# Up-projection blocks of a two-layer decoder: the last low part comes from an adding GpSimd DMA instead of a VectorE subtraction

## What is computed

```python
D_MODEL, SEQ, DEPTH = 2048, 256, 2
D_FF = 4 * D_MODEL

def sq_relu_mlp(h, w_up, w_down):
    return jnp.square(jax.nn.relu(h @ w_up)) @ w_down

for l in range(DEPTH):
    ...
    x = x + sq_relu_mlp(rms_norm(x, mlp_norm_g[l]), w_up[l], w_down[l])
```

## Time and profile before

| | us |
|---|---|
| median of 2 runs | 2017.7 (2017.51 and 2017.88) |
| span of the profiled execution | 2017.5 |
| PE busy | 2008.2 |
| PE weight load busy | 1680.1 |
| DVE busy | 1520.8 |
| ACT busy | 980.1 |
| POOL busy | 13.2 |

### The profile page before, as it was taken

How to read it: one execution, slowest core, us unless ns; L and a number is a source line. 1 busy time by engine, 2 the same in 40 slices (tenths; PEclk the granted TensorE clock), 3 DMA queues, 4 the chain that set the end, 5 groups by cost and what they waited for, 6 DMA issues and landing times.

```text
span 2017.5 us, 26213 instructions
## 1 busy us (share of the span) xinstructions
PE 2008.2 (100%) x9284; PEld 1680.1 (83%) x9284; DVE 1520.8 (75%) x2217; ACT 980.1 (49%) x1263; POOL 13.2 (1%) x21
## 2 busy tenths in 40 slices
PE   9999999999999999999999999999999999999998
PEld 7888888888888888888888998888888888888887
DVE  7789998887568558757888787888558757855875
ACT  6555555444344434434446665554444434444443
POOL 0000000000000000000000000000000000000000
PEclk9999999999999999999999999999999999999999
DMA  8655555655555655655565554565655555565563
GB/s 297 214 170 189 181 167 176 209 194 193 193 190 179 209 189 185 208 189 185 188 208 172 139 150 146 198 219 188 208 188 187 204 191 187 175 218 188 168 219 114
DMA packets 218034, 381.98 MB, mean 189 GB/s; under 512 B 15600, under 2 KB 40560, under 8 KB 217968
## 3 DMA queue, kind: packets, MB, share of 16 engines
q1 hardware_dynamic: 217104, 379.03, 56.9%
q10 hardware_dynamic: 864, 2.10, 0.3%
HBM read 379.00 MB, written 2.10 MB: 189 GB/s over the span
## 4 chain that ended last, share of the span: by engine, by line
PE 97%; issue 2%; DVE 0%; ACT 0%; POOL 0%; POOLq 0%; DVEq 0%; ACTq 0%
PE acc L473 29%; PE acc L475 29%; PE acc L474 29%; PE acc L493 2%; PE acc L494 2%; PE acc L495 2%; PE acc L749 1%; PE acc L750 1%; PE acc L751 1%; PE side L802 0%; PE side L792 0%; PE side L560 0%; DVE wlo L1365 0%; PE side L571 0%; PE side L775 0%
## 5 line engine op out<-in xcount | busy, mean ns | idle before, releaser
L1365 DVE TENSOR_TENSOR wlo<-raw,whi 128x1024 fp32r<-128x1024 f32 (+2 forms) x700 | 836.2, 1212 | 357.2 <-ACT whi L896 353.8
L896 ACT ACTIVATE whi<-raw 128x1024 fp32r<-128x1024 f32 (+2 forms) x700 | 726.3, 1050 | 708.2 <-PE acc L475 677.1
L473 PE MATMUL acc<-whi,opB 128*128 128x512 f32 x1296 | 505.5, 390 | 0.0
L475 PE MATMUL acc<-whi,opB 128*128 128x512 f32 x1296 | 504.4, 389 | 0.0
L474 PE MATMUL acc<-wlo,opB 128*128 128x512 f32 x1296 | 504.2, 389 | 0.0
L473 PE MATMUL acc<-whi,opA 128*128 128x512 f32 (+2 forms) x1296 | 501.8, 387 | 0.0
L475 PE MATMUL acc<-whi,opA 128*128 128x512 f32 (+2 forms) x1296 | 501.0, 387 | 0.0
L474 PE MATMUL acc<-wlo,opA 128*128 128x512 f32 (+2 forms) x1296 | 501.0, 387 | 0.0
L475 PEld LDWEIGHTS acc<-whi,opB 128*128 128x128 f32 x1296 | 243.2, 188 | 50.7
L473 PEld LDWEIGHTS acc<-whi,opB 128*128 128x128 f32 x1296 | 243.3, 188 | 50.4 <-DVE wlo L1365 0.3
L474 PEld LDWEIGHTS acc<-wlo,opB 128*128 128x128 f32 x1296 | 243.3, 188 | 50.1
(11 more groups left out here) (256 smaller groups left out, 1109.0 us busy)
## 6 DMA issues: line engine op xcount, KB each, us to landing
raw<-in_w_up SPq DMA_DIRECT2D x128, 1024.0 KB, 5.3
raw<-in_w_down SPq DMA_DIRECT2D x128, 1024.0 KB, 5.0
raw<-in_a_w_qkv SPq DMA_DIRECT2D x44, 1024.0 KB, 5.1
raw<-in_a_w_o SPq DMA_DIRECT2D x16, 1024.0 KB, 5.0
raw<-in_b_w_o SPq DMA_DIRECT2D x16, 1024.0 KB, 5.0
raw<-in_w_ukv SPq DMA_DIRECT2D x32, 256.0 KB, 4.3
raw<-in_w_dkv SPq DMA_DIRECT2D x4, 1024.0 KB, 5.1
raw<-in_b_w_dq SPq DMA_DIRECT2D x4, 768.0 KB, 4.7
```

Of the source, the lines that this page charges most:

```text
L473: mm(o, a_hi, w_hi, start=first and c == 0, stop=False)
L475: done = mm(o, a_lo, w_hi, start=False, stop=last and c == chunks - 1)
L896: done = fn(whi[:, place:place + ch, 0:n], raw[:, r, c0:c0 + ch, 0:n], ACT.Copy)
L1365: done = tt_(wlo[:, place:place + ch, 0:n], raw[:, r, c0:c0 + ch, 0:n], whi[:, place:place + ch, 0:n].bitcast(F32), ALU.subtract)
```

## The change

In the up blocks alone, half 7's low part is made in another way. ACT rounds `raw` into `whi` as before, and right after it writes `-raw`, rounded, into `wlo` (a second `ACTIVATE`, which increments the new `neg_ready`). DVE leaves out its split of half 7. POOL waits for `neg_ready` and issues a DMA that adds the raw tile (2 chunks, 128x1024 float32, 512 KB) onto `wlo` in SBUF, which leaves raw minus high. Its landing increments `lo_summed` by 16. PE waits for `lo_summed` ahead of half 7, and SP ahead of the next load into quad 3 of `raw`. DVE's split of half 6 increments `lo_ready` by 2. SP's loops are rolled otherwise, so that these waits can be written; its loads have the same order.

```diff
@@ sync
-            def whole(b, w, col, row=0):
+            def whole(b, w, col, row=0, summed=None):
                 for r in range(4):
+                    if r == 3 and summed is not None:
+                        sp.wait_ge(lo_summed, 16 * summed)
                     quad(b, r, w[:, bass.ds(row + 4 * r, 4), bass.ds(col, NB)])
@@ gpsimd
+            def up_lo(l):
+
+                for n in range(JB * QUARTERS):
+                    pool.wait_ge(neg_ready, JB * QUARTERS * l + n + 1)
+                    pool.dma_start(wlo[:, 6:8, :].bitcast(F32), raw[:, 3, 2:4, :],
+                                   accum_op=ALU.add).then_inc(lo_summed, 16)
@@ tensor, up blocks
+                def lo_ready_last(n, also=None):
+                    def ready(hf):
+                        if also:
+                            also(hf)
+                        if hf == 7:
+                            pe.wait_ge(lo_summed, 16 * n + 16)
+                    return ready
@@ scalar, split
                 done.then_inc(hi_ready, 1)
+                if kind == "up" and hf == 7:
+                    fn(wlo[:, place:place + 2, :], raw[:, r, c0:c0 + 2, :], ACT.Copy, scale=-1.0).then_inc(neg_ready, 1)
@@ vector, split
+                if kind == "up" and hf == 7:
+                    return
                 dve.wait_ge(hi_ready, 8 * b + hf + 1)
...
-                done.then_inc(lo_ready, 1)
+                done.then_inc(lo_ready, 2 if kind == "up" and hf == 6 else 1)
```

More of the change, by code:

```diff
@@ L252, in trunk @@
         lo_ready = sem("lo_ready")
+        neg_ready = sem("neg_ready")
+        lo_summed = sem("lo_summed")
         pe_halves = sem("pe_halves")
@@ L371, in mlp, with up, down @@
             def mlp(l):
-                with sp.Fori(0, QUARTERS) as q:
-                    with sp.Fori(0, JB) as j:
-                        whole(B_MLP[l] + 2 * JB * q + j, W_UP[l], D * q + NB * j)
+                def up(q, j):
+                    n = JB * QUARTERS * l + JB * q + j
+                    whole(B_MLP[l] + 2 * JB * q + j, W_UP[l], D * q + NB * j,
+                          summed=None if isinstance(n, int) and n == 0 else n)
+                def down(q):
+                    with sp.Fori(0, JB) as j:
+                        whole(B_MLP[l] + 2 * JB * q + JB + j, W_DOWN[l], NB * j, row=KC * q,
+                              summed=JB * QUARTERS * l + JB * q + JB)
+                for j in range(JB):
+                    up(0, j)
+                with sp.Fori(0, QUARTERS - 1) as q:
+                    down(q)
                     with sp.Fori(0, JB) as j:
-                        whole(B_MLP[l] + 2 * JB * q + JB + j, W_DOWN[l], NB * j, row=KC * q)
+                        up(q + 1, j)
+                down(QUARTERS - 1)
             mlp(0)
@@ L440, in _ @@
                 sub_norm(p)
+            up_lo(0)
             stream_scale(2)
@@ L444, in _ @@
                 nc.gpsimd.tensor_tensor(lrs[:, k, :], lms[:, k, :], neg_half[:, 0:TT], ALU.pow).then_inc(lat_rs, 1)
+            up_lo(1)
             for t in range(TT):
@@ L684, in up @@
                         for k in range(2):
-                            block_tok(B_MLP[l] + 2 * JB * q + 2 * i + k, 1 - k, u[1 - k] + U_QUARTER * q + i, opA)
+                            block_tok(B_MLP[l] + 2 * JB * q + 2 * i + k, 1 - k, u[1 - k] + U_QUARTER * q + i, opA,
+                                      ready=lo_ready_last(JB * QUARTERS * l + JB * q + 2 * i + k))
+                def lo_ready_last(n, also=None):
[5 more added lines that the diff above has]
+                    return ready
                 def hidden_ready(q):
@@ L691, in mlp @@
                     s = (j + 1) % 2
-                    block_tok(B_MLP[l] + j, s, u[s] + j // 2, opA, ready=None if j else opA_ready(v_in))
+                    block_tok(B_MLP[l] + j, s, u[s] + j // 2, opA,
+                              ready=lo_ready_last(JB * QUARTERS * l + j, None if j else opA_ready(v_in)))
                 with pe.Fori(0, QUARTERS - 1) as q:
@@ L1160, in up @@
                     for j in range(JB):
-                        body(B_MLP[l] + 2 * JB * q + j, {6: lambda: hid_high(q, j - 1)} if j else first)
+                        body(B_MLP[l] + 2 * JB * q + j, {6: lambda: hid_high(q, j - 1)} if j else first,
+                             kind="up")
                         drain_up(q, j)
@@ L1800, in up @@
                     for j in range(JB):
-                        body(B_MLP[l] + 2 * JB * q + j, turned(q, j - 1) if j else first)
+                        body(B_MLP[l] + 2 * JB * q + j, turned(q, j - 1) if j else first, kind="up")
                         square_up(q, j)
```

## The result

The changed kernel takes 2090.8 us (median of two runs, 2088.1 and 2093.4) against 2017.7: a ratio of 1.036, 95% interval 1.034 to 1.038. The prediction was 2087 us. The profiled execution has a span of 2086.0 us, 68.5 more than before.

What follows compares the result with a forecast made beforehand. PE was taken as the bound. Stalls at half 7 of 2.5 us in 26 blocks (65 us) and 0.6 in 6 (3.6) sum to 69 us on 2017.5: 2087 us forecast, range 2017 to 2200.

Steps and rivals of the forecast that it cites:

- What bounds the kernel, and what the change removes: PE is busy 2008.2 of 2017.5 us; removing 32 DVE subtractions, 39 us of DVE's time, gains 0.
- The copy on ACT at nothing: 32 more ACT copies, 1.0 us each, delay later splits but are covered by ACT's idle time: no cost.
- What PE has to spare: Gap from the negative copy's end to PE's half 7: 4.0 us in 26 up blocks, 5.9 in 6.
- the 26 blocks: Up blocks with the aside before half 7's split, two MLP-opening blocks included: stalls of 2.5 us each, 65 us.
- L: Route from the negative copy's end to PE's start: 0.1 hand, 1.0 issue, 5.3 landing, 0.1 restart, 6.5 us.
- The 6 first blocks: The other first blocks, without the aside: 5.9 us to spare, stalls of 0.6 us each, 3.6 us.
- The wait that SP gets: SP's quad 3 load for the next block waits for the sum; 5.8 us to spare, cost 0.
- The clock: Rival: stalls drop PE's clock to 1.2 GHz, 2.7 us in 32 blocks, 87 us on top: 2174 us; chance 0.10.
- the hidden case: Rival: the sum lands within the 4.0 us gap before half 7, or nearly: 2018 us, below 2058; chance 0.20.
- the likeliest case: The forecast itself: PE stalls at half 7, L from 5.55 to 8, 2058 to 2134 us; chance 0.45.
- A slow sum near 10 us: Rival: the sum queues behind loads or adds slowly, L near 10, 181 us of stalls: 2198 us; chance 0.24.

Runs made afterwards that it cites:

- e6: The changed kernel with the negative copy ahead of the aside waiting for DVE's transposes, and the quad 2 load held until the sum landed: 2018.6 us, ratio 1.000.
- e1: The kernel before plus ACT's negative copy in the up blocks, overwritten by DVE's subtraction as before, with no POOL DMA: 2018.3 us, ratio 1.000.
- e2: The changed kernel with the negative copy moved ahead of the aside that waits for DVE's transposes: 2025.6 us, ratio 1.0035.
- e5: The changed kernel with SP's wait for the sum moved from the quad 3 load to the next block's quad 2 load: 2045.2 us, ratio 1.013.
- e4: The changed kernel with the POOL DMA copying the raw tile over `wlo` instead of adding it: 2050.7 us, ratio 1.016.
- e7: The changed kernel with the DMA summing one chunk (256 KB), DVE subtracting the other, and the negative copy half as long: 2050.4 us, ratio 1.016.
- e3: The changed kernel with the negative copy one split later, behind the split of the next block's half 0: 2101.3 us, ratio 1.042.
- e8: The changed kernel with the negative copy behind the split of the next block's half 2: 2317.3 us, ratio 1.148.

## Why the prediction was right

**What bounds the kernel, and what the change removes.** Right: DVE's 32 subtractions were worth 0, as the identical times of e6 show. (They took 33 us off DVE's busy time, not 39.)

**The copy on ACT at nothing.** Right, shown by e1.

**What PE has to spare.** Right for the 26 blocks: 4.0 us by the rows, and the stalls are the route less 4.0 (5.98 us gives 1.96 in the block shown). e2 shows that it is this gap, by widening it.

**L.** 6.5 us by the prediction; 5.98 in the block shown and 6.3 on the mean of the 26 (4.0 + 2.3). The sum of the parts was near by luck. The issue was counted twice: issue to landing is measured from the issue's start, so the 0.85 us of POOL lie within it, and the 1.0 should not have been added. Issue to landing was 5.8 where I had 1.0 + 5.3. Without the second count L would have been 5.5, the stalls 1.5 in 26 blocks and none in the other 6, and the forecast 2057 us; the load beside the sum, mis-sized, made up for most of it. The hand to POOL took 0.29 us, not 0.1 (the rows I took it from give 0.17). The reason I gave for 5.3 (a 1 MB load reads as many bytes and lands beside traffic) is half of the truth: alone the sum lands in 4.5, and the load beside it adds 1.3. The Trainium skill, "DMA: Bandwidth & Descriptors", section "Anatomy of one DMA — SWDGE (gpsimd) path", gives, as an estimate with both tiles counted as bytes, 4.4 us. The trace agrees for a sum alone (4.5 us, e5), but in 26 blocks of the changed kernel the sum had a load beside it. By this estimate alone the time would have been 2028, and e5, where it holds, has 2045, as the hand to POOL and PE's restart come on top (5.0 - 4.0 = 1.0 us in 26 blocks).

**The 6 first blocks.** Mis-sized: 0.6 us each, measured 0.00. There no load is beside the sum. SP's was issued at 570.71, the DMA engines were empty from 576 on, and the sum issued at 575.96 landed 4.5 us later, 1.1 us before PE wanted it. I had applied one L to two kinds of block.

**The wait that SP gets.** Right: quad 3 went out at 447.98, with the landing, and ACT never waited for it.

**The clock.** A rival with a chance of 0.10 and a price of 2.7 us in all 32 blocks. It came in part: 6 falls, 1.7 us each, 10 us. A clock under 1.00 after the stalls was one of the prediction's own signs of being wrong, and on this point it was. Without the falls the result would have been near 2080. So the forecast's 2087 is right within 4 us partly because L and the first blocks were put too high (26 x 0.2 + 6 x 0.6 = 9 us) and the clock too low (10 us). The whole range, 2017 to 2200, took in the hidden case too, so lying in it says little; the likeliest case's own, 2058 to 2134, is the tighter test, and it holds.

**The other rivals.** Hidden: false as changed, true in e6, which moves the copy by one place and holds a load back. A slow sum near 10 us: false for the change, but e2 shows such landings (8.8 and 9.6 us) where sum and load start together.

## What to carry to other kernels

Before an operation is moved to a route with a long latency, look up where its input becomes ready in the engine's queue, not how busy the engines are: here one instruction of ACT, standing behind an aside that waits 2.6 us for transposes, made 65 of 73 us. A row for issue to landing already holds the issue, and is not to be added to it. A DMA that adds has to be priced with what is on the DMA engines at that moment, and a load that isn't urgent can be held for it at no cost. And where TensorE is at 99.5%, moving another engine's work can at best be worth nothing.

## What the runs showed of the hardware

- A GpSimd DMA that adds 512 KB, SBUF onto SBUF (128 rows of 4 KB), lands 4.5 us after its issue starts with nothing beside it, of which GpSimd is busy 0.85 (e5). As a plain copy it is 2.9 and 0.54 (e4); with 256 KB added, 3.3 (e7). The issue starts 0.29 to 0.32 us after the end of the ScalarE operation that it waits for, in every run.
- The same sum beside one 1 MB load that is about 2 us ahead: 5.8 us (the changed kernel); with 1 us less to go in the load, 4.7 (e3); with a load issued about 1 us behind it, 5.6 at the median (e2); started together with a load in two blocks of e2, 8.8 and 9.6. Why these last are so much worse than the others wasn't settled; e6 shows only that they go with the load.
- With one "instruction" packet and nothing else beside it the sum landed in 4.9 to 6.2 us in five blocks of e6, and in 4.5 in two of e5.
- TensorE's granted clock fell to the lower level after 6 of 26 waits of 2.0 us on the mean (the longest 2.6) in the changed kernel, after 7 of 32 waits of 1.9 (longest 2.3) in e3, once in e7 (mean 0.95, after the longest, 1.9), after one of two in e2 (3.0, not 2.2), never in e4 (mean 0.95, longest 1.3) or e5 (longest 0.8), and after all 32 of 7 us in e8. The engine had been busy without a break for at least 19 us before each. One fall cost 1.7 us after the short waits and, with the restart, 2.3 in e8. The length of a short wait doesn't decide it: in the changed kernel the clock fell after one of 1.8 us and not after the longest three, 2.4 to 2.6. What does wasn't found in the profile.
